# A fused block kernel: scale and shift of the first norm, order of loads and work up to the values, sums of modulation pieces

## The chip, the cores and the metric

One core of a Trainium2 chip runs the whole program in one launch. The metric is the device time of that launch in microseconds; lower is better. TensorE (PE) multiplies into PSUM, VectorE (DVE), ScalarE (ACT) and GpSimd (POOL) work elementwise, SyncE (SP) issues nearly all DMAs.

## The reference, cut to what matters

Two transformer blocks one after the other on 256 tokens of 1024 features, all in float32; the second puts 16 meta tokens in front. The change touches the beginning of the first block:

```python
cs = jax.nn.silu(c)
mod = cs @ ada_w[l] + ada_b[l]                       # 6 x 1024 values from c (1 x 1024)
shift1, scale1, gate1, shift2, scale2, gate2 = jnp.split(mod, N_MOD, axis=-1)
h = modulate(rmsnorm(x, norm1_g[l]), shift1, scale1) # h * (1 + scale) + shift
proj = h @ w_in[l]
qa, ka, va, qb, kb, vb, ga, gb = jnp.split(proj, offsets, axis=-1)
```

Behind it come window attention of 8 heads (`qa`, `ka`, `va`), causal attention of 8 heads (`qb`, `kb`, `vb`), both gated by sigmoids of `ga`, `gb`, an output projection, an MLP, and then the second block (four gated MLPs, a pooling mixer, a latent attention).

## The kernel before, in words

Activations lie with features on partitions: 8 feature tiles `kt` of 128, with 256 tokens as columns. Float32 matmuls with weights are made of three fast ones: weights and activations are each split into a rounded high part and a low part (the rest), and high x high, high x low and low x high are summed in PSUM.

**The stream of weights.** `weight_plan` cuts all weights into 443 chunks of at most 8 blocks of 128 x 128 (512 KB), in the order of use. `sync_program` (line 511 on) loads chunk `c` into `raw[c % 8]` once chunk `c - 8` is free. A chunk for matmuls is split: ScalarE writes the high part (`split_hi`, line 1009), VectorE the low part (`split_lo`, line 1342), into 5 slots `whi`/`wlo`; a slot is free when TensorE has finished with it. A chunk of `ada_w` is not split: VectorE multiplies it with values of silu(c), one scalar to a partition, and adds up (lines 1362 to 1371, and 1423 for the first stage); TensorE then sums over partitions with a product with a column of ones (line 612 in the first stage, line 600 in `mod_sum`). VectorE adds the bias (line 1376, `mod_out`).

**How far the splits run ahead** is fixed by `Plan`. For the weight chunk in use at stream position `c` it lists the chunks to be split within five positions of the stream; ScalarE goes up to the last of these, VectorE up to the one before it, at least its own:

```python
for i, c in enumerate(self.split):
    ahead = [number[k] for k in range(c, min(c + NRAW - LOADING, len(self.chunks))) if k in number][:AHEAD + 2]
    self.hi_to[i], self.lo_to[i] = ahead[-1], max(i, ahead[-1] - 1)
```

`splits(name)` calls this before a matmul group's own elementwise work.

**First stage.** ScalarE squares x (line 1050); TensorE sums the squares over features with a matrix of 1/1024 (line 619); ScalarE takes the root (1023), VectorE the reciprocal (1386): `rstd`. GpSimd forms y = x * rstd in 8 steps (line 1897). For each tile `kt`, in turn: the products of 8 row blocks of `ada_w` with silu(c), scale and shift side by side (256 columns), the first by ScalarE (1046), seven by VectorE (1423); two sums by TensorE (612); scale and shift values by VectorE (1426, 1427); h = y * gain + shift (ScalarE, 1064), its high part (1066), its low part (VectorE, 1440); the splits of the chunks of `w_in` that this tile needs. TensorE then adds this tile into 13 output tiles of 256 tokens, 39 matmuls (lines 640 to 642), in 7 PSUM banks: the group `qk`. The products of tile `kt + 2` stand ahead of tile `kt`'s splits and low part in VectorE's list.

Meanwhile GpSimd writes the row of position biases to DRAM and at once reads it back as a shifted table for 16 heads (2 MB, line 1899), which the first head needs (`shifts1`, line 1469).

**Values.** `va` (128 columns) and then `vb` (512 columns) are made with tokens on partitions (`token_major`, line 584): 8 tiles x 2 token halves x 3 matmuls each. The qk banks are copied out after the whole qk group. Then `mod_sum("mod4")`.

**Heads.** For head `i` of 16, TensorE's list is: scores of head i, the group `gate{i}` (24 matmuls), transposes of head i-1, values of head i-2. VectorE's list for head i is `shifts1`, a piece of `ada_w` products, `recip1`, `splits("gate{i}")`. Sums of mod5, 8, 9 and 6 stand behind heads 4, 8, 12 and 16; those of mod7, mod10 and mod11 stand behind `wout1`, `mlp_in7` and `mlp_out0`.

## Time and profile before

| | us |
|---|---|
| three runs | 1318.66, 1314.93, 1320.06 (median 1318.66) |
| profiled execution | 1321.37 |
| its span | 1320.0 |
| TensorE busy | 1257.1 (95%) |
| VectorE busy | 894.4 (68%) |
| ScalarE busy | 633.1 (48%) |
| mean granted TensorE clock | 0.974 |

The span is the time from the first to the last recorded work. A matmul is pipelined: its recorded length is longer than the interval to the next, so rates are read from the distance between starts. A product in full float32 shows as two passes. In the chain of waits each piece of time belongs to what the last instruction waited for at that time.

### The profile page before, as it was taken

How to read it: one execution, taken by the hardware profiler on the slowest of the kernel's cores; microseconds unless marked ns; L12 is line 12 of the kernel's file. 1: busy time of each engine (PE TensorE's matmuls, PEld its weight loads, DVE VectorE, ACT ScalarE, POOL GpSimd, SP SyncE). 2: the span in 40 equal slices, each digit the busy share in tenths (PEclk: the TensorE clock that was granted, in tenths of full speed). 3: DMA queues.
4: the chain of work that ended last, by engine and by line, in shares of the span. 5: the costliest groups of instructions: out<-in, count | busy, mean ns of one | idle time of the engine just before them, and what ended most of it. 6: DMA issues, size and time to landing. Idle time of an engine off the chain costs nothing.

```text
span 1320.0 us, 23814 instructions
## 1 busy us (share of the span) xinstructions
PE 1257.1 (95%) x9940; PEld 1221.1 (93%) x9940; DVE 894.4 (68%) x1275; ACT 633.1 (48%) x973; POOL 182.9 (14%) x181
## 2 busy tenths in 40 slices
PE   4999998999999999998799999989999999999996
PEld 3988998999999999998799999989999967999996
DVE  6968878777556766656866656776665563866653
ACT  4545544666444444544544444444454453644531
POOL 2014433000123000012300001400001310000022
PEclk7999999999999999999899999989999987999998
DMA  8956564656555555554245565355556531555540
GB/s 316 381 195 216 192 236 147 242 220 243 194 175 160 177 175 189 177 176 160 88 162 166 182 197 178 131 160 191 190 180 192 190 96 34 176 192 185 185 158 33
DMA packets 66995, 238.88 MB, mean 181 GB/s; under 512 B 7302, under 2 KB 9528, under 8 KB 66888
## 3 DMA queue, kind: packets, MB, share of 16 engines
q1 hardware_dynamic: 66296, 235.17, 53.1%
q0 software_dynamic: 592, 2.19, 0.5%
q8 instruction: 79, 1.29, 0.4%
q14 instruction: 28, 0.23, 0.1%
HBM read 236.26 MB, written 1.07 MB: 180 GB/s over the span
## 4 chain that ended last, share of the span: by engine, by line
PE 85%; DVE 10%; ACT 2%; issue 2%; POOL 1%; DMA 0%; SPq 0%; DVEq 0%; ACTq 0%
PE G L564 25%; PE G L565 25%; PE G L566 25%; DVE sb_wlo L1342 3%; DVE sb_hidf L1423 2%; PE G L584 1%; PE A L666 1%; DVE sb_rstd L1386 1%; PE A L619 1%; PE G L600 0%; DMA sb_X<-in_xT 0%; PE A L689 0%; DVE sb_xl L1843 0%; PE A L584 0%; PE A L676 0%
## 5 line engine op out<-in xcount | busy, mean ns | idle before, releaser
L1342 DVE TENSOR_TENSOR sb_wlo<-sb_raw,sb_whi 128x1024 fp32r<-128x1024 f32 x395 | 488.5, 1270 | 94.0 <-ACT sb_whi L1009 93.7
L564 PE MATMUL G<-sb_xh,sb_whi 128*128 128x256 f32 (+2 forms) x1764 | 503.0, 285 | 12.8 <-DVE sb_gu L1631 7.5
L565 PE MATMUL G<-sb_xl,sb_whi 128*128 128x256 f32 (+2 forms) x1764 | 502.0, 285 | 0.0
L566 PE MATMUL G<-sb_xh,sb_wlo 128*128 128x256 f32 (+2 forms) x1764 | 500.7, 284 | 0.0
L1009 ACT ACTIVATE sb_whi<-sb_raw 128x1024 fp32r<-128x1024 f32 x395 | 404.4, 1050 | 193.5 <-PE G L566 167.7
L564 PEld LDWEIGHTS G<-sb_xh,sb_whi 128*128 128x128 f32 x1764 | 333.8, 189 | 16.5 <-DVE sb_gu L1631 8.4
L566 PEld LDWEIGHTS G<-sb_xh,sb_wlo 128*128 128x128 f32 x1764 | 333.5, 189 | 0.0
L565 PEld LDWEIGHTS G<-sb_xl,sb_whi 128*128 128x128 f32 x1764 | 333.4, 189 | 0.1
L564 PE MATMUL G<-sb_hh,sb_whi 128*128 128x256 f32 (+1 forms) x1056 | 299.5, 284 | 7.1 <-DVE sb_X L1394 4.5
L566 PE MATMUL G<-sb_hh,sb_wlo 128*128 128x256 f32 (+1 forms) x1056 | 298.8, 283 | 0.0
L565 PE MATMUL G<-sb_hl,sb_whi 128*128 128x256 f32 (+1 forms) x992 | 280.3, 283 | 0.0
L564 PEld LDWEIGHTS G<-sb_hh,sb_whi 128*128 128x128 f32 x1056 | 199.2, 189 | 7.8 <-DVE sb_X L1394 4.6
L566 PEld LDWEIGHTS G<-sb_hh,sb_wlo 128*128 128x128 f32 x1056 | 199.2, 189 | 0.0
L565 PEld LDWEIGHTS G<-sb_hl,sb_whi 128*128 128x128 f32 x992 | 186.5, 188 | 0.0
L1193 ACT ACTIVATE sb_gu<-sb_gu 128x272 f32<-128x272 f32 (+1 forms) x88 | 37.4, 425 | 195.8 <-DVE sb_gu L1631 193.2
L1631 DVE TENSOR_TENSOR sb_gu<-G,sb_rstd 128x544 f32<-128x544 f32 (+1 forms) x84 | 59.4, 707 | 62.6 <-PE G L566 62.6
L1871 POOL TENSOR_TENSOR sb_sumsq<-sb_X 128x256 f32<-128x256 f32 (+1 forms) x6 | 3.7, 620 | 699.6 <-DVE sb_X L1394 699.6
L1635 DVE TENSOR_TENSOR sb_hidf<-sb_gu 128x272 f32<-128x272 f32 (+1 forms) x88 | 38.2, 434 | 50.6 <-ACT sb_gu L1193 50.6
L1638 DVE TENSOR_TENSOR sb_hl<-sb_hidf,sb_hh 128x272 fp32r<-128x272 f32 (+1 forms) x88 | 38.2, 434 | 43.2 <-ACT sb_hh L1195 43.2
L1195 ACT ACTIVATE sb_hh<-sb_hidf 128x272 fp32r<-128x272 f32 (+1 forms) x88 | 37.3, 424 | 50.3 <-DVE sb_hidf L1635 50.3
L1876 POOL TENSOR_TENSOR sb_sq<-sb_X 128x256 f32<-128x256 f32 (+1 forms) x42 | 33.0, 787 | 204.7 <-DVE sb_X L1394 204.7
L1879 POOL TENSOR_TENSOR sb_sumsq<-sb_sumsq,sb_sq 128x256 f32<-128x256 f32 (+1 forms) x43 | 47.4, 1102 | 3.4
(300 smaller groups left out, 1299.9 us busy)
## 6 DMA issues: line engine op xcount, KB each, us to landing
sb_raw<-in_wstream SPq DMA_DIRECT2D x443, 512.0 KB, 4.3
sb_bias<-bias_scratch POOLq DMA_DIRECT2D x1, 2048.0 KB, 14.0
sb_X<-in_xT SPq DMA_DIRECT2D x2, 512.0 KB, 6.4
out_T<-sb_X SPq DMA_DIRECT2D x4, 256.0 KB, 2.2
sb_con<-in_consts SPq DMA_DIRECT2D x1, 632.0 KB, 6.6
sb_vec<-in_vecs SPq DMA_DIRECT2D x1, 82.5 KB, 2.0
sb_X<-in_metaT POOLq DMA_DIRECT2D x1, 64.0 KB, 4.6
sb_boh<-in_bias_oh SPq DMA_DIRECT2D x1, 51.0 KB
```

Source lines behind the costliest of these rows:

```text
L564: e.matmul(out, w_h, xs, start=k0 + s.kt == 0, stop=False)
L565: e.matmul(out, w_h, xr, start=False, stop=False)
L566: m = e.matmul(out, w_l, xs, start=False, stop=k0 + s.kt == ktotal - 1)
L1009: e.activation(whi[:, i % NSPLIT, 0:w], raw[:, c % NRAW, 0:w], ACT.Copy).then_inc(hi_done, 1)
L1193: e.activation(gu[:, b, 0, 0:n], gu[:, b, 0, 0:n], ACT.Silu).then_inc(silu_done, 1)
L1195: e.activation(hh[:, j * n:(j + 1) * n], hidf[:, b, 0:n], ACT.Copy).then_inc(hid_hi, 1)
L1342: e.tensor_tensor(wlo[:, i % NSPLIT, 0:w], raw[:, c % NRAW, 0:w], f(whi[:, i % NSPLIT, 0:w]), ALU.subtract).then_inc(lo_done, 1)
L1631: e.tensor_tensor(gu[:, b, :, 0:n], G[plan.pair[name]][:, :, 0:n], rb, ALU.mult).then_inc(left_dve, 1)
L1635: e.tensor_tensor(hidf[:, b, 0:n], gu[:, b, 0, 0:n], gu[:, b, 1, 0:n], ALU.mult).then_inc(hid_mul, 1)
L1638: e.tensor_tensor(hl[:, sl], hidf[:, b, 0:n], f(hh[:, sl]), ALU.subtract).then_inc(hid_lo, 1)
L1876: e.tensor_tensor(s, src, src, ALU.mult).then_inc(sumsq_done, 1)
L1879: e.tensor_tensor(sumsq[:, cols], sumsq[:, cols], s, ALU.add).then_inc(sumsq_done, 1)
```

## The change

- `ada_w` for scale and shift of tiles 0 and 1 comes as four chunks `ada_p{kt}_{i}` (eight row blocks of one of the two), and TensorE multiplies them with silu(c) directly (`shift_scale_direct`). Tiles 2, (3, 4), (5, 6), 7 are `UNITS`; for a pair VectorE's products have 512 columns.
- Scale and shift values are formed by ScalarE. The squares are added by VectorE first and summed by one matmul. `rstd` is exp(-0.5 ln(mean + eps)), both on ScalarE.
- The order of chunks is: ada_p0_1, ada_p0_0, ada_p1_1, ada_p1_0, ada_h2_0, qk_0, ada_h2_1, qk_1, qk_2, four of unit (3, 4), qk_3 to 5, four of unit (5, 6), qk_6 to 8, two of unit (7,), qk_9 to 12; then ada4_0, v_0 to v_2, ada4_1, v_3 to v_5, ada4_2, v_6, v_7, ada4_3, ada5_0, gate0, ada5_1, gate1.
- The values are one group `v` of 5 blocks to a tile (8 chunks of 5 blocks), made in two halves of 320 columns.
- qk banks are copied out as each is finished. GpSimd forms y before it stores the bias row, and reads the table back only once the low part of qk chunk 11 is done.
- `mod_sum` transposes the four accumulated blocks; `mod_out` sums them over the columns and adds the bias. The third matmul of a head's values goes into the first.

The core of the diff (names of semaphores, PSUM places and copies left out):

```diff
+    def some_qk(n):
+        for i in range(done[0], done[0] + n):
+            group(f"qk_{i}", qk[i * CH:(i + 1) * CH], True)
+        done[0] += n
+
+    def unit(tiles):
+
+        per = CH // (2 * len(tiles))
+        for m in range(KT // per):
+            group(f"ada_h{tiles[0]}_{m}", [("ada_w", 0, _r(r * P), _r((i * KT + kt) * P)) for r in _r(per * m, per) for kt in tiles for i in (1, 0)], True)
+
+    for kt in range(PE_TILES):
+        for i in (1, 0):
+            group(f"ada_p{kt}_{i}", [("ada_w", 0, _r(r * P), _r((i * KT + kt) * P)) for r in range(KT)], True)
+    unit(UNITS[0])
+    groups.insert(len(groups) - 1, ("qk_0", qk[:CH], True))
+    done[0] = 1
+    some_qk(2)
...
+    unit(UNITS[1])
...
+    some_qk(3)
...
+    v_group = lambda kt: group(f"v_{kt}", [("w_in", 0, _r(kt * P), c) for c in [_r(o["va"])] + [_r(o["vb"] + j * P) for j in range(4)]], True)
+    for part, kts in enumerate(((0, 1, 2), (3, 4, 5), (6, 7), ())):
         ada(4, part)
-    group("va", [("w_in", 0, _r(kt * P), _r(o["va"])) for kt in range(KT)], True)
-    for part in (2, 3):
-        ada(4, part)
-    group("vb", [("w_in", 0, _r(kt * P), _r(o["vb"] + j * P)) for kt in range(KT) for j in range(4)], True)
+        for kt in kts:
+            v_group(kt)
...
@@ -597,60 +622,81 @@
                     if t % 4 == 0:
                         e.wait_ge(ada_total, ADA_ORDER.index(i + t // 4) + 1)
                     acc = ada_sets[ADA_SET[i + t // 4]][0][:, t % 4 * P:(t % 4 + 1) * P]
-                    m = e.matmul(out[:, 0, t:t + 1], acc, one_col[:, 0:1], start=True, stop=True)
+                    m = e.transpose(out[:, 0, t * P:(t + 1) * P], acc, ident)
...
+            def shift_scale_direct(kt):
+
                 if kt:
                     e.wait_ge(gain1_done, 2 * kt)
                 else:
-                    e.wait_ge(root_done, ROOT["norm1"])
-                for n in range(2):
...
-                    m = e.matmul(A[0][:, n:n + 1], acc1(kt)[:, n * P:(n + 1) * P], one_col[:, 0:1], start=True, stop=True)
+                    e.wait_ge(silu_c, 1)
+                for i in (1, 0):
+                    c = where[f"ada_p{kt}_{i}"][0][0]
+                    e.wait_ge(loaded[c % NRAW], 16 * (c // NRAW + 1))
+                    for r in range(KT):
+                        m = e.matmul(A[0][:, 1 - i:2 - i], raw[:, c % NRAW, r * P:(r + 1) * P], csil[:, r:r + 1], start=r == 0, stop=r == KT - 1)
+                    m.then_inc(sum1_half, 1)
+
+            def shift_scale_sum(u):
+
+                e.wait_ge(acc1_done, products_to(u, KT - 1))
+                e.wait_ge(gain1_done, 2 * UNITS[u][0])
+                for n in range(2 * len(UNITS[u])):
+                    m = e.matmul(A[0][:, n:n + 1], acc1(u)[:, n * P:(n + 1) * P], one_col[:, 0:1], start=True, stop=True)
                 m.then_inc(sum1_done, 1)
...
+            src1 = lambda kt: (xh[:, kt, COLS1], xl[:, kt, COLS1])
+            shift_scale_direct(0)
             e.wait_ge(consts_set, 5)
+            e.wait_ge(xsum_done, 4)
+            mean(0, COLS1, None, 1)
+            shift_scale_direct(1)
+            e.wait_ge(rows_in, 32)
+            e.matmul(G[1][0:HEADS1, 1, 0:BIASC], brow[:, :], boh[:, :], start=True, stop=True).then_inc(bias_made, 1)
+
+            sums_at = {(1, 0): 0, (2, 9): 1, (4, 9): 2, (6, 6): 3}
+            for s in steps["qk"]:
+                kt = s.kt
+                if (kt, s.t) in sums_at:
+                    shift_scale_sum(sums_at[kt, s.t])
+                if s.t == 0:
+                    e.wait_ge(xl_done, XSTAGE["h"] + kt + 1)
+                if (kt, s.t) == (0, 9):
+                    e.wait_ge(bias_row, 1)
+                if s.opens:
+                    e.wait_ge(lo_done, s.i + 1)
...
+                    m.then_inc(qk_bank, 1)
+                m = e.matmul(out, w_l, xh[:, kt, COLS1], start=False, stop=kt == KT - 1, skip_group_check=True)
+                if s.closes or s.j == QK_TILES * KT - 1:
...
+                s, last = steps["v"][5 * kt], steps["v"][5 * kt + 4]
+                e.wait_ge(lo_done, s.i + 1)
+                w_h, w_l = (w[:, s.i % NSPLIT, 0:640] for w in (whi, wlo))
+                for i in range(2):
+                    rows = slice(META + i * P, META + (i + 1) * P)
+                    for half in range(2):
+                        if kt == 0 and half == 0:
+                            e.wait_ge(qk_act, i + 1)
+                        elif kt == 0:
+                            e.wait_ge(qk_dve, i + 1)
+                        cols, out = slice(320 * half, 320 * half + 320), v_out[i][half]
+                        e.matmul(out, xh[:, kt, rows], w_h[:, cols], start=kt == 0, stop=False)
+                        e.matmul(out, xl[:, kt, rows], w_h[:, cols], start=False, stop=False)
+                        m = e.matmul(out, xh[:, kt, rows], w_l[:, cols], start=False, stop=kt == KT - 1)
+                m.then_inc(mm_done, 1)
             e.wait_ge(qk_act, 4)
             e.wait_ge(qk_dve, 3)
+            e.wait_ge(con_in, 16)
             mod_sum("mod4", 4)
 
...
-                e.matmul(o[:, P:SEQ], vv(0), pT1[:, b, 0:P], start=True, stop=False)
-                e.matmul(o[:, P:SEQ], vv(1), pT1[:, b, P:SEQ], start=False, stop=True)
-                e.matmul(o[:, 0:P], vv(0), pT1[:, b, SEQ:384], start=True, stop=True).then_inc(valued1, 1)
+                e.matmul(o[:, 0:SEQ], vv(0), pT1[:, b, 0:SEQ], start=True, stop=False, skip_group_check=True)
+                e.matmul(o[:, P:SEQ], vv(1), pT1[:, b, SEQ:384], start=False, stop=True, skip_group_check=True).then_inc(valued1, 1)
...
-            e.activation(warm[:, 1:2], eps_c[:, 0:1], ACT.Sqrt)
...
+            e.activation(warm[:, 1:2], eps_c[:, 0:1], ACT.Ln)
...
+            def shift_scale(kt, n=0):
+                e.activation(g1m[:, kt:kt + 1], A[0][:, 2 * n:2 * n + 1], ACT.Identity, bias=gb[:, kt:kt + 1], scale=V("norm1_g", kt)).then_inc(gain1_done, 1)
+                e.activation(mod[:, kt:kt + 1], A[0][:, 2 * n + 1:2 * n + 2], ACT.Identity, bias=V("ada_b", kt)).then_inc(gain1_done, 1)
+
...
+            for n in range(4):
+                e.wait_ge((x_in, x_rest)[n // 2], 16)
+                e.activation(sig[:, 2 * n:2 * n + 2, :], X[:, 2 * n:2 * n + 2, COLS1], ACT.Square).then_inc(xsq_done, 1)
+            e.wait_ge(gb_done, 1)
+            e.wait_ge(sum1_half, 2)
+            shift_scale(0)
+            e.wait_ge(mean_done, MEAN["norm1"])
+            e.activation(root[:, COLS1], A[1][:, 0:SEQ], ACT.Ln, bias=eps_c[:, 0:1]).then_inc(root_done, 1)
+            preload(ACT.Exp)
+            e.wait_ge(root_done, ROOT["norm1"])
+            e.activation(rstd[:, COLS1], root[:, COLS1], ACT.Exp, scale=-0.5).then_inc(rstd_done, 1)
+            split_hi(0)
+            x_high(0)
+            split_hi(1)
+            e.wait_ge(sum1_half, 4)
+            shift_scale(1)
+            x_high(1)
+            e.wait_ge(bias_made, 1)
+            e.activation(brows[:, :], G[1][0:HEADS1, 1, 0:BIASC], ACT.Copy).then_inc(bias_row, 1)
+            split_hi(2)
+            first_product(1)
+            unit_shift_scale(0)
+            x_high(2)
+            split_hi(5)
+            first_product(2)
+            unit_shift_scale(1)
+            x_high(3)
+            x_high(4)
+            split_hi(8)
+            first_product(3)
+            unit_shift_scale(2)
+            x_high(5)
+            x_high(6)
+            split_hi(10)
+            unit_shift_scale(3)
+            x_high(7)
+            split_hi(13)
...
+            qk_copy(0)
+            split_hi(14)
+            qk_copy(2)
+            split_hi(15)
+            qk_copy(4)
+            qk_copy(6)
+            splits("v")
+            e.wait_ge(mm_done, ended["v"])
+            e.activation(vtok[:, 0, 0:320], A[2][:, 0:320], ACT.Copy).then_inc(v0_act, 1)
+            e.activation(vtok[:, 1, 0:320], G[plan.pair["v"]][:, 0, 0:320], ACT.Copy).then_inc(left_act, 1)
...
-                e.tensor_tensor(mod[:, 4 * i:4 * (i + n)], G[plan.pair[name]][:, 0, 0:4 * n], V("ada_b", 4 * i, 4 * n), ALU.add).then_inc(left_dve, 1)
+                e.tensor_reduce(mod[:, 4 * i:4 * i + 4], G[plan.pair[name]][:, 0, :].rearrange("p (t d) -> p t d", t=4), AX_X, ALU.add).then_inc(left_dve, 1)
+                e.wait_ge(left_dve, plan.left_dve[name])
+                e.tensor_tensor(mod[:, 4 * i:4 * i + 4], mod[:, 4 * i:4 * i + 4], V("ada_b", 4 * i, 4), ALU.add).then_inc(mod_set, 1)
...
+            for n in range(1, 4):
+                e.wait_ge(xsq_done, n + 1)
+                if n > 1:
+                    e.wait_ge(xsum_done, n - 1)
+                e.tensor_tensor(sig[:, 0:2, :], sig[:, 0:2, :], sig[:, 2 * n:2 * n + 2, :], ALU.add).then_inc(xsum_done, 1)
+            e.wait_ge(xsum_done, 3)
+            e.tensor_tensor(sumsq[:, COLS1], sig[:, 0, :], sig[:, 1, :], ALU.add).then_inc(xsum_done, 1)
+            e.wait_ge(silu_c, 1)
+            products(0, 0, 4)
+            split_lo(0)
+            x_low(0)
+            split_lo(1)
+            products(0, 4, 8)
+            x_low(1)
+            split_lo(2)
+            products(1, 1, 4)
+            split_lo(3)
+            x_low(2)
+            products(1, 4, 8)
+            split_lo(5)
+            x_low(3)
+            x_low(4)
+            split_lo(6)
+            products(2, 1, 4)
+            split_lo(7)
+            products(2, 4, 8)
+            split_lo(8)
+            x_low(5)
+            x_low(6)
+            products(3, 1, 8)
+            split_lo(9)
+            split_lo(10)
+            x_low(7)
+            split_lo(12)
...
-            for part in (0, 1):
-                ada_piece(4, part)
-            split_lo(plan.lo_to[steps["va"][0].i])
-            e.wait_ge(mm_done, ended["qk"])
-            for i in (1, 3, 5):
-                qk_copy(i)
-            splits("va")
-            for part in (2, 3):
-                ada_piece(4, part)
-            splits("vb")
-            e.wait_ge(mm_done, ended["vb"])
-            e.tensor_copy(vtok[:, 1, P:5 * P], G[plan.pair["vb"]][:, 1, :]).then_inc(left_dve, 1)
+            ada_piece(4, 0)
+            split_lo(13)
+            qk_copy(1)
+            qk_copy(3)
+            split_lo(14)
+            qk_copy(5)
+            split_lo(15)
+            ada_piece(4, 1)
+            split_lo(18)
+            ada_piece(4, 2)
+            split_lo(20)
+            ada_piece(4, 3)
+            splits("v")
+            e.wait_ge(mm_done, ended["v"])
+            e.tensor_copy(vtok[:, 0, 320:640], A[3][:, 0:320]).then_inc(v0_dve, 1)
+            e.tensor_copy(vtok[:, 1, 320:640], G[plan.pair["v"]][:, 1, 0:320]).then_inc(left_dve, 1)
             mod_out("mod4")
...
+            e.wait_ge(rstd_done, RSTD["norm1"])
+            for kt in range(KT):
+                e.tensor_tensor(sig[:, KT + kt, :], X[:, kt, COLS1], rstd[:, COLS1], ALU.mult).then_inc(y_done, 1)
             e.wait_ge(bias_row, 1)
             e.dma_start(scratch[:, 0:BIASC], brows[:, :]).then_inc(rows_out, 16)
             hankel = bass.AP(scratch.tensor, 0, [[1, P], [512, HEADS1], [1, SEQ]])
-            e.wait_ge(rstd_done, RSTD["norm1"])
```

## Rows read from the trace of the kernel before

**Rows 1.** the page: busy time and share of each engine, DMA issues.

```profile
...
PE 1257.1 (95%) x9940; PEld 1221.1 (93%) x9940; DVE 894.4 (68%) x1275; ACT 633.1 (48%) x973; POOL 182.9 (14%) x181
...
sb_bias<-bias_scratch POOLq DMA_DIRECT2D x1, 2048.0 KB, 14.0
...
```

**Rows 2.** the chain of waits, 0 to 120 us: start us, us, what.

```profile
...
2.12 5.92 DMA sb_X<-in_xT
...
8.85 6.65 PE A L619 x16
...
57.66 0.39 PE G L640
71.66 5.31 PE A L584 x48
76.97 11.17 PE G L584 x48
88.14 0.79 PE G L600 x8
...
```

**Rows 3.** TensorE's instructions: start us, us, line, operation, out<-in, [idle before <-releaser].

```profile
...
16.17 0.61 PE L612 MATMUL A<-sb_one_col,sb_hidf 128*128 128x1 f32 x4
...
27.68 0.58 PE L640 MATMUL G<-sb_xh,sb_whi 128*128 128x256 f32 x1 [1.52 <-DVE sb_xl L1440]
...
69.34 0.28 PE L640 MATMUL A<-sb_xh,sb_whi 128*128 128x256 f32 x1
...
71.38 0.28 PE L642 MATMUL A<-sb_xh,sb_wlo 128*128 128x256 f32 x1
...
```

**Rows 4.** VectorE's instructions, 0 to 93 us.

```profile
...
16.04 1.75 DVE L1386 RECIPROCAL sb_rstd<-sb_root 128x256 f32<-128x256 f32 x1 [1.03 <-ACT sb_root L1023]
...
18.77 6.00 DVE L1423 SCALAR_TENSOR_TENSOR sb_hidf<-sb_raw,sb_csil,sb_hidf 128x256 f32<-128x256 f32 x7 [0.82 <-ACT sb_hidf L1046]
...
24.95 2.34 DVE L1342 TENSOR_TENSOR sb_wlo<-sb_raw,sb_whi 128x1024 fp32r<-128x1024 f32 x2
...
27.55 3.66 DVE L1423 SCALAR_TENSOR_TENSOR sb_hidf<-sb_raw,sb_csil,sb_hidf 128x256 f32<-128x256 f32 x7
...
```

**Rows 5.** ScalarE's instructions, 0 to 93 us.

```profile
...
15.53 0.47 ACT L1023 ACTIVATE sb_root<-A,sb_eps_c 128x256 f32<-128x256 f32 x1 [4.29 <-PE A L619]
...
16.78 1.28 ACT L1019 ACT_TABLE_LOAD   x1
...
20.47 0.58 ACT L1064 ACTIVATE sb_tmp<-sb_sig,sb_mod,sb_g1m 128x256 f32<-128x256 f32 x1
21.09 0.42 ACT L1066 ACTIVATE sb_xh<-sb_tmp 128x256 fp32r<-128x256 f32 x1
...
```

**Rows 6.** groups by line, 0 to 93 us: count | busy us, mean ns.

```profile
...
L1897 POOL TENSOR_TENSOR sb_sig<-sb_X,sb_rstd 128x256 f32<-128x256 f32 x8 | 6.6, 858 | 0.1
...
L1365 DVE SCALAR_TENSOR_TENSOR sb_gu<-sb_raw,sb_csil,sb_gu 128x512 f32<-128x512 f32 x6 | 4.1, 746 | 0.0
...
```

**Rows 7.** windows: length, busy us (count) of each engine, granted clock, DMA share, GB/s.

```profile
...
15.00:20.00 5.00, 2.63 (x13) 1.52 (x11) 3.12 (x6) 4.17 (x7) 2.81 (x4) 0.83 1.03 409
...
25.00:30.00 5.00, 3.30 (x15) 3.25 (x16) 4.79 (x9) 1.53 (x3) 0.67 (x1) 0.50 0.83 255
...
216.00:218.00 2.00, 2.00 (x13) 2.00 (x12) 1.92 (x2) 0.31 (x1) 1.92 (x3) 0.56 0.50 203
...
348.00:350.00 2.00, 2.00 (x19) 2.00 (x19) 1.68 (x3) 2.00 (x4) 1.92 (x4) 1.00 0.03 8
...
```

**Rows 8.** the chain of waits, 84 to 98 us: start us, us, what.

```profile
...
89.81 0.42 DVE sb_sc L1469
...
94.12 0.39 PE G L564
...
```

**Rows 9.** TensorE after the sums of mod7 and mod11.

```profile
...
214.87 0.39 PE L564 MATMUL G<-sb_hh,sb_whi 128*128 128x256 f32 x1 [1.97 <-DVE sb_X L1394]
...
347.78 0.38 PE L564 MATMUL G<-sb_hh,sb_whi 128*128 128x256 f32 x1 [2.51 <-DVE sb_X L1394]
...
```

198 lines of the change are left out of this document (76 added, 122 removed).

## The prediction, as put on record before the changed kernel was run

> **What bounds the kernel now.** Read first the shares: TensorE is busy 95% of the span [rows 1]. Time is won only where TensorE idles or does work it could spare. The chain of waits over the first 120 us shows where that is: x lands at 8.0, TensorE sums squares until 15.5, and then the chain is VectorE's until 57.7; from there it is TensorE back to back: qk to 71.7, va 5.3 us, vb 11.2 us, sums of mod4 0.8 us, first scores [rows 2]. TensorE's first qk matmul is at 27.7, at the half clock [rows 3, 7]. From 27.7 to 71.5 are 43.8 us; 312 matmuls at 0.120 (17 intervals from 69.34 to 71.38 [rows 3]) are 37.4, the rest is slow clock and waits for VectorE. Each feature tile costs VectorE seven products, one or two low splits and an x low part [rows 4].
>
> **The start.** The direct sums of tile 0 read raw chunks 0 and 1. ScalarE used chunk 0 at 5.0; I start there. A one-column product is two passes: four passes took 0.61 with their tail [rows 3], 0.11 each warm, about 0.22 cold. The 16 matmuls of the squares ran at 0.42 a pass [rows 2], twice the 0.21 I expect of the full clock, though the clock column reads 1.00; so TensorE is cold until some 5.7 us into its first work. 32 passes: done at 11.7. The squares end at 10.6 as before; VectorE's four adds (0.6 each, 0.35 the last) end at 11.9; the mean is now two passes: 12.5. Ln 0.5, table load 1.3, warm 0.1, Exp 0.5 [rows 5]: rstd at 15.0, against 17.8 (sqrt, then 1.75 of reciprocal [rows 4]). Tile 1's direct sums (3.5) and the bias matmul run under that, until 17.
> Table load: the trace has one between square root and the next Exp [rows 5], so I charge 1.3. (The Trainium skill, "ScalarE: Activation LUTs", section "Table sets: the hidden batching unit", says one set holds both ln and exp, so one load serves both; by that rstd stands at 13.7 and all behind it up to 1.3 earlier. No row here shows that set.)
> GpSimd forms y in eight steps of 0.83 while VectorE works. VectorE's seven products beside it took 6.0, without it 3.66 [rows 4]: +0.33 an operation. Seven VectorE operations now fall beside it: +2.3. (The Trainium skill, "SBUF — State Buffer", section "Who interferes with whom", has a VectorE operation with two SBUF inputs and a GpSimd one exclude each other for a whole instruction. 0.49 and 0.83 in turn would be 1.3 a product; the row shows 0.84, so the trace does not bear out full exclusion. By the rule the start would lose some 3 us more.)
> With y0 at 15.8, high split 1.0, two steps of x high 1.04 [rows 5], low split 1.15 [rows 4] and x low 0.35, plus 0.5 of the above: qk starts at 18.3, 9.4 earlier.
>
> **The qk stage**, walked in the order written. A step (tile, three matmuls) 0.355; low split 1.15; product of 512 columns 0.76 (0.746 busy [rows 6], dependent), of 256 columns 0.51 [rows 4]; x high 1.04, to TensorE 1.5; shift/scale on ScalarE 0.2 an operation; a sum 0.5 a tile.
> - kt 0: 18.3 to 23.0. VectorE: low 1 to 19.8, products(0,4..8) at 0.84 to 23.1, x low 1, low 2 to 24.65. kt 1 starts 23.65, reaches low 3 at 27.5, which is done at 28.1 behind three products: idle 0.6.
> - kt 2: low 4 is queued behind products(1,4..8) (28.4 to 31.5): 32.65, wanted at 31.0: idle 1.7. Sum 1 stands at tile 9 (0.95); kt 2 ends 36.1. x high 3 cannot start before that sum: x low 3 at 36.9, idle 0.8.
> - kt 3, 4: low 6, 7 in time; sum 2 at (4,9) waits for products(2) (46.2): idle 1.4; then x high 5: 0.85.
> - kt 5: low 9 is behind seven products of the last unit: these start at 50.4 after x low 6, end 54.0, low 9 at 55.2; wanted at 51.9: idle 3.3.
> - kt 6, 7: sum 3 at 60.0, x high 7, high 11, low 11 at 63.7; wanted 61.4: idle 2.3. End of qk 69.5.
> 51.2 us: 37.4 of matmuls, 2.9 of sums, 10.9 idle, where before 43.8 held 6.4 of sums, slow clock and idle. Against 71.5: **-2.0**. Bounds: TensorE without any wait would end at 18.3+37.4+2.4=58 (-13), but VectorE's 34 us of this list plus the handovers don't allow it; I keep 4 us either way.
> Loads: 512 KB at 409 GB/s [rows 7] is 1.28. A chunk is asked for eight back: 14 when products(0) end (23.1), 20 when products(1) end (31.5), 25 at 42: each lands 3 to 4 us later, before ScalarE wants it. The bias table (2 MB, 14.0 us to landing [rows 1], during which the weights came at 255 GB/s [rows 7]) no longer takes bandwidth here: that removes a wait of ScalarE of 7 us, part of the old stalls. It now starts at 63.7 and lands by some 80; wanted at 85. Costed at nothing; without that margin it is one for one.
>
> **Values.** 96 matmuls before: 48 of 128 columns in 5.3, 48 of 512 in 11.2 [rows 2]: 0.111 and 0.232. Now 96 of 320. Between 256 columns (0.120) and 512 the time goes with columns, 0.452 ns each: 0.145, in all 13.9 against 16.5: **-2.6** (bounds 0.111 and 0.232 each: -5.8 to +5.8; the neighbours on both sides fix it). Chunks of five blocks cost the splits 0.8 instead of 1.15; VectorE is 3 us ahead. The copies of qk run in the last kt.
>
> **Sums of mod pieces.** Eight passes become four transposes: 0.79 to 0.9 [rows 2] down to 0.44. Mod4: **-0.45**. In the head stage TensorE is the bound: mod5, 8, 9, 6 **-1.8**; VectorE's +0.75 (a 512-column reduction, a wait, an add) replaces idle time there. Mod7, 10 and 11 stand before a residual or evacuation that TensorE awaits (2.5 us at mod11 [rows 9]): -0.45+0.75 each, **+0.9**. Values of two matmuls in place of three: same columns, 0.
>
> **Head 0: the new wait.** VectorE's low splits run ahead to lo_to: the last weight chunk within five stream chunks, less one. Before, the last vb chunk (37) saw gate0 (39) and gate1 (41): gate0's low part was done during vb. Now the stream ends v7 (39), ada4_3, ada5_0, gate0 (42), ada5_1, gate1 (44): v7 sees only gate0, lo_to is v7 itself. So gate0's low split stands behind shifts1(0), an ada piece and recip1(0). Before, the split of gate1 stood there: shifts began at 89.81, that split released TensorE at 94.12, 4.3 later [rows 8]. TensorE's queue is scores1(0), gate0, scores1(1), gate1, transposes; all wait. Shifts also start 0.5 later (two copies 0.9, reduction 0.65, add 0.16 against 0.97). Idle 4.8, less the 0.55 that gate1 cost: **+4.25**. The bound below is 0 (if the split runs ahead after all).
>
> **Clock.** The granted clock fell to 0.5 around the idle time at 17 to 27 and again at 216 after a wait of 2.0 us; after the 2.5 us at mod11 it did not [rows 7, 9]. From 27.7 it took 3.9 us of work to come back: 2.0 us lost. For the 4.8 us of head 0 I take **+2.0** (bounds 0 and 3.4). For the 3.3 of kt 5 perhaps 1.7, which I set against the table load that may go.
>
> **Sum.** -2.0 -2.6 -0.45 -1.8 +0.9 +4.25 +2.0 = **+0.3**. The profiled run took 1321.37 (span 1320.0, 1.4 around it), 2.7 above the median of 1318.66 of the three runs; the difference carries over: 1321.7 profiled, **1319.0** as a median.
>
> **Rivals.**
> 1. *The early start is kept.* If VectorE and ScalarE hand over better than I walk (one table load, waits at kt 2 and kt 5 half as long), qk ends 5 to 6 earlier: 1312, with a warm clock 1311. For: 11 us of idle rest on my placing of products; against: the placing is the written order. 0.18.
> 2. *No stall at head 0.* Then -4.25 -2.0: 1312.7. Against: the lo_to rule above. 0.07.
> 3. *Slower: the clock.* TensorE now has gaps of 1.7, 3.3, 2.3 and 4.8, plus 1.3 before kt 0. Each that drops the clock costs up to 2.0, and behind each late sum stands ScalarE. Four drops with little slack: +8 against +2: about 1326. It decides from the third drop on (over +6.6). For: one drop after 2.0 us idle; against: none after 2.5. 0.10.
> 4. *The bias table lands late*: it shares the queues with v3 to v7; 1 us per us beyond 85; 8 us late would give 1327. 0.03.
> 5. *GpSimd and VectorE take whole turns* at the start: 7 operations at 0.49+0.83 instead of 0.84 are 3.4 more: 1322.4. The products beside y speak against it [rows 4]. 0.02. (This is the SBUF page's rule above.)
> 6. *One table load serves both*: 1317.7, a variant inside the forecast, 0.4 of it. (The ScalarE page's rule above.)
> 7. *It changes less than it says* (gain in qk near 0, rest as above): 1321, inside the forecast's own case.
> The forecast, with 6 and 7, has 0.60. About 0.5% (6.6 us) is what a measurement can tell from no change. Below 1312.1: most of rival 1 and half of 2, 0.18; above 1325.3: 0.11; between 0.71. Range: 1311 to 1325.
>
> **What would show it.** qk's first matmul near 18.3; rstd 15.0 (13.7 without a load); gaps at low 4, low 9, low 11 with VectorE's split as releaser; qk's end 69.5; v matmuls 0.145 apart; first scores near 84; then TensorE idle 4 to 5 us before gate0, released by the low split; clock 0.5 behind it. Wrong if gate0 follows the scores at once, if qk ends before 66 or after 73, or if a DMA releases ScalarE's splits for long.

## The result: 0.8% slower, outside the range

| kernel | median us (lowest to highest, runs) | profiled execution, its span | mean clock |
|---|---|---|---|
| before | 1317.42 (1314.93 to 1320.06, 4) | 1321.37, 1320.0 | 0.974 |
| changed | 1328.72 (1326.36 to 1333.02, 4) | 1329.67, 1328.0 | 0.977 |

Ratio 1.0082, 95% interval 1.0053 to 1.0111: some 11 us slower. Forecast were 1319.0 with a range of 1311 to 1325. A second measurement of both kernels side by side (experiment 11) gave 1327.68 against 1318.07, ratio 1.0073 (1.0057 to 1.0089).

### The profile after

TensorE's share is unchanged, and the bias table takes as long to land as before [rows 1]:

```profile
...
PE 1260.1 (95%) x9918; PEld 1227.0 (92%) x9918; DVE 890.5 (67%) x1247; ACT 634.8 (48%) x988; POOL 185.9 (14%) x181
...
sb_bias<-bias_scratch POOLq DMA_DIRECT2D x1, 2048.0 KB, 14.0
...
```

TensorE at the start (start us, us, then line, operation, out<-in, and in brackets the idle time before it). In the kernel before, the squares and the first qk matmul stand in [rows 2, 3]:

```profile
...
5.29 6.96 PE L639 MATMUL A<-sb_csil,sb_raw 128*128 128x1 f32 x32 [5.29 <-DMA sb_raw<-in_wstream]
12.29 1.19 PE L617 MATMUL A<-sb_sumsq,sb_mean_ones 128*128 128x256 f32 x2
13.28 6.83 PE L639 MATMUL A<-sb_csil,sb_raw 128*128 128x1 f32 x32
20.03 1.46 PE L657 MATMUL G<-sb_boh,sb_brow 34*16 34x384 f32 x2
21.42 0.58 PE L672 MATMUL A<-sb_xh,sb_whi 128*128 128x256 f32 x1
...
```

Both groups of 32 one-column passes (the direct sums of tiles 0 and 1, direct(0) and direct(1)) take 0.21 us a pass, the second no faster than the first. TensorE has no idle time from 5.29 on, so its queue sets the start: qk begins at 21.42, 6.3 earlier than before. The elementwise work for it was done at 19.27 (the low part of x, on VectorE). The granted clock is full only from 25.7, so tile 0 of qk runs mostly at the half clock.

ScalarE at the root [rows 5]. The table load stands between Ln (L1120) and Exp (L1123):

```profile
...
13.52 0.47 ACT L1120 ACTIVATE sb_root<-A,sb_eps_c 128x256 f32<-128x256 f32 x1 [0.67 <-PE A L617]
14.02 1.28 ACT L1066 ACT_TABLE_LOAD   x1
15.42 0.40 ACT L1123 ACTIVATE sb_rstd<-sb_root 128x256 f32<-128x256 f32 x1
...
```

GpSimd's eight products beside VectorE, where before one took 858 ns [rows 6] (a group by line: count | busy us, mean ns | idle before it):

```profile
...
L2012 POOL TENSOR_TENSOR sb_sig<-sb_X,sb_rstd 128x256 f32<-128x256 f32 x8 | 8.2, 1064 | 15.4 <-ACT sb_rstd L1123 15.4
...
```

Six of the eight took 0.72 to 0.92 us, as all eight did before. The two others took 1.71: they ran while VectorE made the low parts of chunks 0 and 1, of which the first took 1.60 us in place of 1.21.

TensorE's waits from there on, in order ("low 4" is the wait for VectorE's low part of qk chunk 4): low 4, low 9, low 11, the end of v with the sum of mod4 and the first scores, gate0 in head 0, the output projection, the sum of mod7 and what follows it, what follows the sum of mod10, and what follows the sum of mod11 [rows 2, 8, 9]. Two of 0.8 to 0.9 us, at 51.1 and 54.5, are left out:

```profile
...
37.17 0.39 PE L672 MATMUL G<-sb_xh,sb_whi 128*128 128x256 f32 x1 [1.65 <-DVE sb_wlo L1429]
...
60.53 0.58 PE L672 MATMUL G<-sb_xh,sb_whi 128*128 128x256 f32 x1 [3.26 <-DVE sb_wlo L1429]
...
72.05 0.39 PE L672 MATMUL G<-sb_xh,sb_whi 128*128 128x256 f32 x1 [2.42 <-DVE sb_wlo L1429]
...
93.42 0.60 PE L625 MATMUL G<-sb_con,sb_gu 128*128 128x128 f32 x4
93.95 0.70 PE L712 MATMUL A<-sb_qk 64*128 64x256 f32 x2
...
99.63 0.55 PE L589 MATMUL G<-sb_xh,sb_whi 128*128 128x256 f32 x1 [4.76 <-DVE sb_wlo L1429]
...
216.13 0.36 PE L589 MATMUL G<-sb_hh,sb_whi 128*128 128x256 f32 x1 [1.90 <-DVE sb_wlo L1429]
...
223.36 0.60 PE L625 MATMUL G<-sb_con,sb_sc 128*128 128x128 f32 x4
...
226.18 0.39 PE L589 MATMUL G<-sb_hh,sb_whi 128*128 128x256 f32 x1 [2.23 <-DVE sb_X L1483]
...
287.62 0.39 PE L589 MATMUL G<-sb_xh,sb_whi 128*128 128x258 f32 x1 [1.65 <-DVE sb_hidf L1696]
...
359.85 0.39 PE L589 MATMUL G<-sb_hh,sb_whi 128*128 128x256 f32 x1 [3.25 <-DVE sb_X L1483]
...
```

Windows around four of them, as in [rows 7] (length; busy us and count of TensorE, its weight loads, VectorE, ScalarE, GpSimd; granted clock; DMA share, GB/s):

```profile
...
38.00:42.00 4.00, 4.00 (x26) 3.90 (x25) 0.68 (x2) 2.62 (x9) 0.00 (x0) 0.67 0.91 327
...
59.00:67.00 8.00, 6.47 (x31) 6.47 (x32) 2.61 (x3) 0.00 (x0) 0.00 (x0) 0.57 0.70 254
97.00:104.00 7.00, 4.37 (x20) 4.40 (x21) 3.13 (x6) 2.86 (x7) 3.46 (x2) 0.53 0.54 162
...
360.00:363.00 3.00, 3.00 (x16) 3.00 (x17) 2.64 (x4) 2.16 (x5) 2.92 (x4) 0.54 0.00 0
...
```

Every wait shown but one has half clock (1.2 GHz) at it or behind it: 3.4 us from 39.4, 6.8 from 59.9, 3.4 from 73.5, 6.8 from 97.4, then 3.4 each from 216.9, 227.1 and 360.2. The wait of 1.65 us at 287.6 has none.

VectorE in head 0 shows why gate0 waits. The ada piece (L1449) and the reciprocal (L1606) run before the two low splits, of gate0 and gate1:

```profile
...
96.67 0.88 DVE L1449 TENSOR_SCALAR sb_hidf<-sb_raw,sb_csil 128x512 f32<-128x512 f32 x2
...
98.19 0.17 DVE L1606 RECIPROCAL sb_stat<-sb_stat 128x2 f32<-128x2 f32 x1
98.28 2.34 DVE L1429 TENSOR_TENSOR sb_wlo<-sb_raw,sb_whi 128x1024 fp32r<-128x1024 f32 x2
...
```

Where the time went is read from the starts of the same operations in every profile: VectorE's evacuation of the scores of heads 0 and 1, the first and third residual tile after attention (between them stands mod7's sum), the first residual tile behind the sums of mod10 and mod11, and the first gated product of the layer behind that, in us:

| profile | scores 0 | scores 1 | resid 0 | resid 2 | resid 8 | gated 0 |
|---|---|---|---|---|---|---|
| before | 89.81 | 93.99 | 208.32 | 213.94 | 346.86 | 434.99 |
| before again (8) | 88.91 | 93.09 | 207.43 | 213.05 | 345.96 | 435.67 |
| changed | 95.23 | 105.64 | 218.17 | 225.26 | 358.93 | 448.63 |
| changed again (11) | 93.94 | 104.25 | 216.76 | 223.86 | 357.51 | 447.83 |
| 1 gate0 ahead | 95.30 | 100.16 | 214.02 | 221.11 | 354.79 | 444.49 |
| 2 wide matmuls | 95.90 | 105.59 | 218.09 | 224.42 | 358.09 | 448.40 |
| 3 late order | 85.30 | 95.14 | 207.63 | 214.73 | 348.40 | 437.94 |
| 4 rest alone | 86.88 | 91.74 | 205.72 | 212.81 | 346.50 | 436.20 |
| 5 late, gates, sums | 85.71 | 89.77 | 202.26 | 207.88 | 340.75 | 430.45 |
| 6 high 3 ahead | 84.78 | 88.61 | 201.09 | 207.84 | 340.74 | 430.46 |
| 12 the same again | 84.04 | 88.09 | 200.55 | 206.17 | 338.95 | 428.67 |
| 7 rest, best | 87.20 | 91.03 | 203.56 | 210.27 | 343.19 | 432.90 |
| 9 bias first | 85.62 | 89.45 | 201.91 | 207.55 | 340.44 | 430.16 |
| 10 gates only | 85.21 | 89.26 | 201.76 | 208.88 | 342.54 | 432.82 |
| 13 warm, bridged | 82.60 | 86.43 | 198.91 | 204.52 | 337.41 | 427.12 |

The changed kernel against the one before: 5.4 us lost by the first scores, 6.2 in head 0, 1.8 regained over the heads, 1.5 lost between resid 0 and resid 2, 0.8 at mod10 and mod11 together, and 1.6 in the half clock at 360. Not all of the 1.5 is mod7's sum: the half clock from 216.9 to 220.3 stands ahead of that sum (223.36), behind the wait of 1.90 us at 216.13, which the kernel before has as well, without half clock behind it. Experiment 2 has the same sum with no half clock there, and loses 0.7 (6.33 us from resid 0 to resid 2, against 5.62 before and 7.09 in the changed kernel):

```profile
...
221.78 0.60 PE L625 MATMUL G<-sb_con,sb_sc 128*128 128x128 f32 x4
...
225.35 0.39 PE L589 MATMUL G<-sb_hh,sb_whi 128*128 128x256 f32 x1 [2.97 <-DVE sb_X L1489]
...
```

In all the changed kernel is 13.6 us later at gated 0, more than the 11 of the medians. From gated 0 to the end the kernel before took 885.0 us in its first profile and 877.5 in its second, the changed kernel 879.4 and 881.2, so differences behind that point are not the change's.

### The profile page after: what moved, and what is told of

It reads as the page before. It is cut to its first block, busy times and chain, and to the rows that moved or that the text cites. A ratio compares the mean times of both kernels' runs of the same rounds, so it can differ in the third digit from the quotient of the medians.

```text
span 1328.0 us, 23775 instructions
## 1 busy us (share of the span) xinstructions
PE 1260.1 (95%) x9918; PEld 1227.0 (92%) x9918; DVE 890.5 (67%) x1247; ACT 634.8 (48%) x988; POOL 185.9 (14%) x181
## 3 DMA queue, kind: packets, MB, share of 16 engines
q8 instruction: 78, 1.28, 0.4%
## 4 chain that ended last, share of the span: by engine, by line
PE 82%; DVE 9%; ACT 2%; issue 2%; POOL 1%; DVEq 0%; ACTq 0%
PE G L589 25%; PE G L590 25%; PE G L591 25%; DVE sb_wlo L1429 2%; DVE sb_rstd L1475 1%; PE A L737 1%; PE A L712 1%; ACT sb_whi L1056 1%; DVE sb_xl L1961 0%; ACT sb_p L1392 0%; DVE sb_X L1824 0%; PE A L589 0%; PE A L723 0%; PE G L1007 0%; POOL sb_sumsq L1997 0%
## 5 line engine op out<-in xcount | busy, mean ns | idle before, releaser
L1429 DVE TENSOR_TENSOR sb_wlo<-sb_raw,sb_whi 128x1024 fp32r<-128x1024 f32 (+1 forms) x398 | 489.1, 1262 | 97.9 <-ACT sb_whi L1056 97.7
L1056 ACT ACTIVATE sb_whi<-sb_raw 128x1024 fp32r<-128x1024 f32 (+1 forms) x398 | 404.5, 1043 | 183.0 <-PE G L591 169.7
```

Of the source, the lines that this page charges most:

```text
L1056: e.activation(whi[:, i % NSPLIT, 0:w], raw[:, c % NRAW, 0:w], ACT.Copy).then_inc(hi_done, 1)
L1429: e.tensor_tensor(wlo[:, i % NSPLIT, 0:w], raw[:, c % NRAW, 0:w], f(whi[:, i % NSPLIT, 0:w]), ALU.subtract).then_inc(lo_done, 1)
```

## The experiments

Ratios are to the kernel before on the same chip, with 95% intervals; chips differ between experiments (1 to 4, 5 to 12, 13), so compare the ratios rather than the times across these groups. Line numbers are the experiment's own.

**1. gate0's low split ahead.** In VectorE's program:

```
...
             splits("v")
+            split_lo(21)
...
```

> The changed kernel with one more low split on VectorE before it waits for the values (the low part of gate0). Theory A (the split queued behind head 0's softmax costs the 10.4 us between the first two score evacuations, 4.8 of them idle and the rest half clock): that distance falls to about 4.2, the total by 6.2 to 6.7 us, and the clock column shows no 0.5 at 97 to 104. Rival: head 0 is bound by the chain shift, exponential, reciprocal anyway; then TensorE idles before gate1 instead and the total falls by 2 at most.

Measured: 1326.32 us, ratio 1.0052 (1.0034 to 1.0070). The stall before gate0 is gone, but now gate1 waits:

```profile
...
100.30 0.58 PE L589 MATMUL G<-sb_xh,sb_whi 128*128 128x256 f32 x1 [1.72 <-DVE sb_wlo L1429]
...
```

with the clock at half for 3.4 us from 100. The second scores follow the first by 4.86 us (10.41 in the changed kernel, about 4.2 expected); of the 6.2 us, 4.2 came back by resid 0. The ratio fell by 0.3%, some 4 us, less than the 6.2 to 6.7 expected. The cause of the stall is shown; it had a second wait right behind it.

**2. Wide matmuls for the clock.** Five of 384 columns ahead of the direct sums, four behind the bias matmul, their result unused.

> The changed kernel with wide filler matmuls (128x384 float32, result not used): 5 before the direct sums, 4 between the bias row and the first qk matmul. Theory B (TensorE stayed at half clock through 64 one-column passes and kt 0, and that made qk late): qk starts by 19.5 instead of 21.4, kt 0 runs at 0.12 a matmul instead of 0.21, kt 1 starts at 24.6 instead of 28.6, the first score evacuation 4 us or more earlier than 95.2. Rival (the handovers of VectorE and ScalarE bound the stage): kt 1 starts 4 earlier but the gaps at low 4 and low 9 grow by as much, and the first scores come at most 1.5 earlier. Open: whether the one-column passes run at 0.11 once the wide ones have raised the clock, or fall back to 0.21.

Measured: 1330.92 us, ratio 1.0101 (1.0071 to 1.0130).

```profile
...
1.40 4.89 PE L654 MATMUL G<-sb_mean_ones 128*128 128x384 f32 x10 [1.40 <-DVE sb_mean_ones L1502]
6.12 3.63 PE L639 MATMUL A<-sb_csil,sb_raw 128*128 128x1 f32 x32
12.10 1.22 PE L617 MATMUL A<-sb_sumsq,sb_mean_ones 128*128 128x256 f32 x2 [2.35 <-DVE sb_sumsq L1532]
13.12 6.83 PE L639 MATMUL A<-sb_csil,sb_raw 128*128 128x1 f32 x32
...
21.26 4.55 PE L654 MATMUL G<-sb_mean_ones 128*128 128x384 f32 x8
25.35 0.57 PE L678 MATMUL A<-sb_xh,sb_whi 128*128 128x256 f32 x1
...
```

Behind wide work direct(0)'s passes take 0.11 us. Then TensorE idles 2.35 us for VectorE's adds, the clock falls, and it stays at half for 13.7 us from 11.1, though TensorE works without a break from 12.10, for 6.8 us of that in one-column passes. So the clock fell in an idle stretch, and direct(1) ran its whole length at half. The last fillers ran at half clock and pushed qk to 25.35 (19.5 expected), which ate the gain: the first scores come at 95.90, no earlier. Whether the handovers would have eaten it otherwise, the rival, this run cannot say.

**3. Order of the late tiles.** ScalarE takes high 12 where it took high 10; VectorE takes low 9 between the products of the last unit:

```
...
-            x_low(5)
-            x_low(6)
-            products(3, 1, 8)
-            split_lo(9)
-            split_lo(10)
+            products(3, 1, 5)
+            x_low(5)
+            x_low(6)
+            split_lo(9)
+            products(3, 5, 8)
+            split_lo(12)
...
```

> The changed kernel with another order at tiles 5 to 7 alone: four products of the last unit before x low 5, low 9 before the remaining three, high and low parts of chunks 11 and 12 before tile 7's scale and shift. Theory C (the idle 3.3 us before low 9 and 2.4 before low 11, and the half clock from 60 to 66.7 behind the first, come from the order alone): both gaps go, no slow stretch there, first score evacuation 7 to 8 us earlier (about 87.5). Rival (the clock falls anyway or the last unit's sum, wanted at tile (6,6), now waits for the products): 3 us or less.

Measured: 1320.11 us, ratio 1.0002 (0.9982 to 1.0022); first scores 9.9 us earlier than in the changed kernel.

```profile
...
58.00:66.00 8.00, 8.00 (x70) 8.00 (x70) 6.27 (x9) 3.74 (x9) 1.21 (x1) 1.00 0.99 363
...
```

TensorE is busy throughout that window, at the full clock. The two gaps were 3.26 and 2.42 us, 5.7 together. The other 4.2 fit the half clock behind them. From the start of kt 5 to the end of qk the changed kernel takes 24.99 us (54.52 to 79.51), this one 14.60 (54.99 to 69.59). Of the 10.4 between them 5.7 are the two waits; the rest is 4.7, and an estimate of what the 10.2 us of half clock cost is 4.8 (half of the 9.6 in which TensorE was busy). This one order was most of the loss: the ratio falls from 1.0082 to 1.0002.

**4. The rest of the change, with the first stage of before.** V in halves of 320 columns, chunks of five blocks, qk banks copied out as they end, transposed sums, two matmuls for a head's values, gate0's split ahead.

> The kernel before with the other parts of the change and without its first-stage order: values in halves of 320 columns, five-block chunks, qk banks copied out as they end, sums of mod pieces by transposes, two matmuls for a head's values; gate0's low part ahead as in e1. The forecast's terms for these parts: -2.6 values, -0.45 mod4, -1.8 and +0.9 for the other sums: 3.5 to 4 us below the kernel before, first score evacuation at 87.3 (89.8 before, of which +0.5 for VectorE's longer end of stage). If the first-stage order is what made the change slower, this one is faster than before; if the values or sums did, it is not.

Measured: 1318.21 us, ratio 0.9996 (0.9978 to 1.0014). First scores at 86.88 (87.3 expected), 2.9 earlier than in the first profile of before and 2.0 earlier than in its second; of the 2.9, 2.2 are lost by the scores of head 4, at gate1 and the half clock behind it, and what stands behind the heads gives back more. The expected gain of 3.5 to 4 us in the time is not there: the interval holds 1.

**5. Three mends together:** the order of 3; gate0 as in 1 and gate1's parts likewise (ScalarE's high part before the first exponentials, VectorE's low part behind the first shifts); mod7, 10 and 11 summed by one-column products again. In head 0, `recip1` also stands ahead of the `ada_w` piece.

```
...
-                    m = e.transpose(out[:, 0, t * P:(t + 1) * P], acc, ident)
+                    if i in (7, 10, 11):
+                        m = e.matmul(out[:, 0, t:t + 1], acc, one_col[:, 0:1], start=True, stop=True)
...
                     shifts1(i)
-                    ada_piece(*ADA_HEADS[i])
-                    recip1(i)
+                    if i == 0:
+                        split_lo(22)
+                        recip1(i)
+                        ada_piece(*ADA_HEADS[i])
...
```

> The changed kernel with four edits, each aimed at a wait its trace shows: the late-tile order of the third experiment; the low split of gate0 straight behind the v splits and, new, gate1's (ScalarE's high part ahead of the first exponentials, VectorE's low part straight behind the first shifts); and mod7, mod10 and mod11 again summed by one-column products with one add. Theory (the loss is handovers, each doubled by the half clock behind it): against the late-order kernel the stall in head 0 goes, with the clock drop behind it (-6.2 us), and the three sums that stand before a waiting evacuation give back 1 us each (-3.0 to -3.4, the half clock behind mod7 included). Against the kernel before, the first scores stay 4.5 us earlier, the fourth head's are 4 to 5 us earlier, and mod10's evacuation is 6 to 8 us earlier: 1311 to 1313 us, ratio 0.994 to 0.996. Rival A (TensorE's late stages take back what the start gains, whatever the handovers): ratio 0.999 to 1.001. Rival B (the clock falls in these stages whatever stands in front of it): the stall is gone, but half-clock stretches still stand near 90, 205 and 350 us; 1315 to 1317 us.

Measured: 1314.65 us, ratio 0.9989 (0.9966 to 1.0011). In head 0 VectorE now does:

```profile
...
87.15 1.22 DVE L1433 TENSOR_TENSOR sb_wlo<-sb_raw,sb_whi 128x1024 fp32r<-128x1024 f32 x1
...
88.76 1.08 DVE L1453 TENSOR_SCALAR sb_hidf<-sb_raw,sb_csil 128x512 f32<-128x512 f32 x2
...
```

and head 1's scores follow head 0's by 4.06 us (10.41 in the changed kernel, 4.18 before). The profile has 6.1 us less than before at resid 0, and still at resid 8. The medians keep 2.5 of it, with an interval that reaches past 1: the stages behind vary by several us (8). The 1311 to 1313 us expected are missed, and the ratio is within 0.0001 of rival A's range. Rival B is borne out in part: near 90 no half clock is left, but stretches of 3.4 us still stand at 208.8 and 341.9, behind waits of 1.96 and 2.52 us that the kernel before has too.

**6. High split 3 ahead** of the shift and scale of tile 2, on ScalarE.

> The previous kernel, and ScalarE takes the high part of chunk 3 before the shift and scale of tile 2 instead of behind it. Theory (VectorE's idle time near 28 us and TensorE's wait at low split 4 near 37 us come from that high part standing behind a wait for the sum): VectorE's 2.9 us of idle shrink, TensorE's gap of 1.65 us goes, and if the clock drop near 38 us was answered by that gap it goes too: 2 to 4 us less than the previous kernel, 1308 to 1311. Rival (the gap only moves: x high 3 and the sum of unit 0 then come late by as much): within 1 us of the previous kernel.

Measured: 1312.82 us, ratio 0.9971 (0.9959 to 0.9983). The gap of 1.7 us before low 4 and the half clock behind it are gone, and the values start 2.3 us earlier than in 5 (66.98 against 69.28). Yet the first scores come only 0.9 earlier, and the median 1.8, with intervals that overlap; expected were 2 to 4. Where the rest goes the profile shows:

```profile
...
80.95 1.06 ACT L1059 ACTIVATE sb_whi<-sb_raw 128x1024 fp32r<-128x1024 f32 x1 [3.09 <-DMA sb_raw<-in_wstream]
...
82.04 1.23 DVE L1434 TENSOR_TENSOR sb_wlo<-sb_raw,sb_whi 128x1024 fp32r<-128x1024 f32 x1 [1.27 <-ACT sb_whi L1059]
83.18 0.48 DVE L1585 COPY sb_vtok<-A 128x320 f32<-128x320 f32 x1
...
```

The values end at 81.54, but VectorE copies them only at 83.18: gate0's low split, now ahead of the copies, waits for gate0's weights, with the DMA share at 1.03 and 408 GB/s from 74 to 81. With the early stage mended, the loads are the next limit there.

This profile also has half clock from 199.6, which 5 has not, behind the same gap:

```profile
...
199.05 0.36 PE L589 MATMUL G<-sb_hh,sb_whi 128*128 128x256 f32 x1 [1.89 <-DVE sb_wlo L1434]
...
199.00:203.00 4.00, 3.95 (x21) 3.98 (x22) 3.76 (x6) 1.40 (x4) 1.28 (x2) 0.58 1.00 379
...
```

and in 5:

```profile
...
200.22 0.35 PE L589 MATMUL G<-sb_hh,sb_whi 128*128 128x256 f32 x1 [1.89 <-DVE sb_wlo L1433]
...
200.00:204.00 4.00, 3.78 (x32) 3.81 (x33) 3.75 (x7) 1.40 (x4) 1.12 (x2) 1.00 0.95 370
...
```

**7. The first stage of before, with the rest in its mended form** (4 with the gate1 and the sums of 5). "The first kernel of this call" is that of 5.

> The first stage exactly as in the kernel before (root by Sqrt and reciprocal, all sums by accumulated products, its loads); behind it all the rest of the change: v in halves of 320 columns, chunks of five blocks, transposed sums for mod4, 5, 8, 9, 6, values of two matmuls, with the gates and mod7, mod10, mod11 mended as in the first kernel of this call. Theory: first scores 2.9 us earlier than before (as measured with the fourth experiment), the gap before gate1 and its half clock gone (-2.5), mod5, 8, 9, 6 -1.8, nothing given back at mod7, 10, 11: 5 to 7 us under the kernel before at mod10, 1312 to 1315 us. Set against the first kernel of this call it gives what the new first stage is worth with its order mended: the theory says 0 to 2 us. Rival (the new first stage is a gain of several us once its order is right): this kernel at 1316 or more with the first one at 1312.

Measured: 1315.57 us, ratio 0.9980 (0.9960 to 1.0001). Against 5 at resid 0 the new first stage is worth 1.3 us (0 to 2 expected), against 6 it is 2.5. In the medians it is 0.9 and 2.8, with overlapping intervals, so its worth in the time is not shown.

**8. The kernel before, once more.**

> The kernel before, unaltered, for a second profile of it. Question: do its half-clock stretches stand at the same places. Theory (a stretch is answered by what the kernel does there): again 13.7 us at 18, 3.4 at 216, 10.2 at 626, 6.8 at 872; none near 227 or 348. The stretch of 27 us at 1080, twice to four times as long as in all kernels since, is chance and will be 7 to 17 us here. Rival (the stretches are drawn by chance everywhere): different places all through.

Measured: 1314.53 us (one run). The early stretches are near where they were (19.7, 214.3, 623.9, 873.0), the first of them shorter (10.2 us, not 13.7), with one more, from 347.4, that was not expected; the one of 27 us is 3.4 us, less than the 7 to 17 expected. Windows of the first profile of before, then of the second:

```profile
...
347.00:350.00 3.00, 2.22 (x19) 2.22 (x20) 2.44 (x5) 2.57 (x5) 2.43 (x4) 1.00 0.02 5
...
1085.00:1105.00 20.00, 20.00 (x63) 11.61 (x62) 9.12 (x29) 6.93 (x19) 0.00 (x0) 0.50 0.18 53
...
```

```profile
...
347.00:350.00 3.00, 3.00 (x16) 3.00 (x17) 2.62 (x4) 2.18 (x5) 2.92 (x4) 0.57 0.03 5
...
1085.00:1105.00 20.00, 17.50 (x103) 12.70 (x102) 10.33 (x32) 7.78 (x20) 0.00 (x0) 0.91 0.20 55
...
```

So the half clock behind mod11's sum (1.6 us) is no mark of the change, and a single profile can be off by several us: 0.9 by the first scores (88.91 against 89.81) and 7.5 behind gated 0.

**9. Bias row first.** Its inputs are loaded first and its matmul stands ahead of the direct sums; the copies out of the pair bank go first.

> The sixth experiment's kernel (late-tile order, gates ahead, three column sums, high split 3 ahead) with two more edits: the bias row's small inputs are loaded first and its matmul stands before the direct sums, in TensorE's idle first 5 us, instead of between direct(1) and the first qk matmul (1.4 us there); and both engines copy the half of v that lies in the pair bank first, since gate0 waits for that bank (1.3 us of idle before gate0). Theory (the start is bound by TensorE's queue, and gate0 by the order of two copies): first qk matmul at 20.0 to 20.3 in place of 21.4, gate0's first matmul 0.4 us closer to the scores, 1 to 2 us off the time against the sixth kernel: 1311 to 1312, ratio to before 0.995 to 0.9965. Rival (VectorE sets the pace right behind: low split 3, the product sums): the first 1.4 us are gone again by tile 3, and the time is within 0.5 us of the sixth kernel's.

Measured: 1311.45 us, ratio 0.9947 (0.9932 to 0.9962), beside 1313.49 for 12 on the same chip; the intervals overlap. The mechanism did not work: the small loads landed only by 4.44, the direct sums began at 5.83, the mean at 14.09 (12.29 in the changed kernel), and qk began at 21.76, no earlier (20.0 to 20.3 expected). The other edit did what it should: TensorE idles 0.35 us before gate0, where it was 1.34 in 6 and 0.65 in 12. The first scores come later than in 6 and 12. So the median is where it was expected, but not by the mechanism named for the start: that is luck, and whether the 2 us against 12 are the edits' doing stays open. It is the fastest median of all, and clearly below the kernel before and the changed one.

**10. Gates and order, transposed sums kept** (5 without its sums).

> The changed kernel with the late-tile order and both gates ahead, all modulation sums by transposes as in the change: the fifth experiment's kernel less its three column sums. Theory (a transposed sum is 0.45 us cheaper where TensorE is the bound, but costs VectorE 0.75 us more where an evacuation is awaited): up to mod6 the same as the fifth kernel; then later by 1.0 to 1.5 us at mod7 (some of it the clock), 0.4 at mod10, 0.4 at mod11, in all 2 to 3.5 us, ratio to before 0.999 to 1.001. Rival (the three sums matter only through the clock's chance): within 1 us of the fifth kernel in the stretches between the clock's drops.

Measured: 1315.99 us, ratio 0.9979 (0.9968 to 0.9990). From 0.5 us ahead of 5 at resid 0 it falls 1.0 behind at resid 2, 1.8 at resid 8, 2.4 at the gated product: 2.9 in all. Only about half of it is the three sums'. Of the 1.5 by resid 2, 0.8 is the half clock from 200.1, ahead of mod7's sum, behind a wait of 1.90 us that 5 has too, without it; mod10 and mod11 cost 0.8; the last 0.6 is a difference that the two profiles of the changed kernel show as well (89.70 and 90.32 us from resid 8 to gated 0). And the ratio is no higher than that of 5 (0.9979 against 0.9989), where more was expected: the time does not show the sums. What one sum costs is seen in the idle time behind mod11's:

```profile
...
343.46 0.58 PE L589 MATMUL G<-sb_hh,sb_whi 128*128 128x256 f32 x1 [3.24 <-DVE sb_X L1484]
...
```

against 2.52 in 5. The 0.72 more is VectorE's longer evacuation; TensorE's sum is 0.35 shorter (0.60 against 0.95).

**11 and 12. The changed kernel and 6, again, on one chip.**

> The changed kernel itself once more, on the same chip as the others of this call, with a second profile. Theory: 1326 to 1329 us, ratio 1.007 to 1.009; first scores 5.4 us later than before, the second head's scores another 6.2 us; half-clock stretches again at the gaps before low split 9 and in head 0, while those far behind (at 227 and 360) may be elsewhere or missing, since the two profiles of the kernel before differ there as well. Rival (the stretch at 60 was chance): it is missing and the first scores come 2 to 3 us earlier.

> The sixth experiment's kernel once more, beside the first kernel of this call and beside the changed kernel on one chip. Expected 1312 to 1314 us, ratio to before 0.996 to 0.998, 14 to 16 us under the changed kernel. Against a ratio of 1.000 or more the gains seen in its first profile would be the profile's chance.

Measured: 1327.68 us, ratio 1.0073 (1.0057 to 1.0089), and 1313.49 us, ratio 0.9969 (0.9952 to 0.9986). All seven early stretches of half clock of the changed kernel are there again; only their lengths differ at low 4 (6.8 us, not 3.4) and low 9 (3.4, not 6.8). The first scores are 5.0 later than in before's second profile (expected 5.4), the second 6.1 more. Both medians are where they were expected; the kernel of 6 is 14.2 us under the changed one.

**13. A warm TensorE without idle time:** 6 with wide matmuls ahead of direct(0), between it and the mean, and behind the bias row.

```
...
+            wide_fill(5)
             shift_scale_direct(0)
...
+            wide_fill(4)
...
+            wide_fill(3)
...
```

> The sixth experiment's kernel with wide matmuls (384 columns, their result unused) wherever TensorE would idle before the first qk matmul: five ahead of the direct sums (in its idle first 5 us), four between direct(0) and the mean, three behind the bias matmul. In the second experiment the five in front made direct(0)'s 32 passes run at 0.11 us in place of 0.21, but TensorE then idled 2.35 us, the clock fell at 11.1, and direct(1) ran at 0.21 again. Theory (the forecast's start at 18.3 failed only because nothing wide kept TensorE at the full clock): both direct sums at 0.11 a pass, direct(1) done at 16.5, bias 0.7 more, first qk matmul at 18.6 to 19.3 and all of kt 0 at 0.12: kt 0 ends at about 24, 4 us earlier than in the sixth kernel; of that VectorE's later handovers leave 1 to 3 us at the first scores (81.5 to 83.5). Rival A (one-column passes lose the full clock even with no idle time around them): direct(1) at 0.21 in part, first qk matmul at 20 to 22, the last three fillers slow: 0 to 2 us later than the sixth kernel. Rival B (VectorE sets the pace from tile 1 on): kt 0 ends 4 us earlier, kt 1 or kt 2 waits for it, and the first scores stand within 0.5 us of the sixth kernel's 84.0 to 84.8.

Measured: 1313.98 us, ratio 0.9972 (0.9943 to 1.0002).

```profile
...
6.41 3.63 PE L642 MATMUL A<-sb_csil,sb_raw 128*128 128x1 f32 x32
9.90 2.83 PE L657 MATMUL G<-sb_mean_ones 128*128 128x384 f32 x8
12.56 0.69 PE L617 MATMUL A<-sb_sumsq,sb_mean_ones 128*128 128x256 f32 x2
13.09 3.63 PE L642 MATMUL A<-sb_csil,sb_raw 128*128 128x1 f32 x32
17.76 0.81 PE L666 MATMUL G<-sb_boh,sb_brow 34*16 34x384 f32 x2 [1.05 <-DMA sb_brow<-in_bias_rows]
18.51 3.86 PE L657 MATMUL G<-sb_mean_ones 128*128 128x384 f32 x6
21.91 0.57 PE L682 MATMUL A<-sb_xh,sb_whi 128*128 128x256 f32 x1
...
```

Both direct sums now run at 0.11 a pass, the second done at 16.7, as the prediction had it (17 with the bias row). So one-column passes do not lose the full clock by themselves (rival A). Then the bias row's load is late, the clock falls at 18.5, and the last fillers take 3.9 us: qk begins at 21.91, not at 18.6 to 19.3. x low 0 was done at 19.15. Even so the first scores come at 82.60 (81.5 to 83.5 expected), 1.4 to 2.2 earlier than in 12 and 6. A gain in the median is not shown.

## Why the prediction was wrong, step by step

- **The start: failed first.** "TensorE is cold until some 5.7 us into its first work", then 0.11 a pass: that carried the first 32 direct passes to 11.7 and TensorE's queue to 17, ahead of the elementwise chain, from which 18.3 for qk was worked out. Measured were 0.21 a pass throughout: the chain was ready at 19.27, the queue only at 21.42. The clock stayed at half until 25.7, so kt 0 and its sum took 6.98 us where 5.35 were forecast. I had taken the change from 0.42 to 0.21 among wide matmuls and applied it to passes of one column, which had stood at the half clock, 0.21, all along (2). With wide work ahead and no idle time, the forecast rate appears (13).
- **rstd** at 15.0, measured 15.8, of which 0.5 is the mean at the half clock (1.19 us, against 0.69 in 13); the table load was charged, rightly. (The Trainium skill, "ScalarE: Activation LUTs", section "Table sets: the hidden batching unit", has ln and exp in one set. The trace does not agree: a load of 1.28 us stands between them.)
- **GpSimd beside VectorE**: forecast 0.84 us a product; the four beside it took 0.94, 0.77, 0.77 and 0.77 (L1514), and started 0.86 to 1.05 apart, not the 1.3 of whole turns. Rival 5 did not happen. The low splits were another case: there GpSimd took 1.71 us, and the split 1.60.
- **The gaps at low 4, low 9, low 11**: forecast 1.7, 3.3, 2.3; measured 1.65, 3.26, 2.42. For these the walk through the written order was good to 0.12 us. All waits of qk together were forecast at 10.9 and came to 9.0.
- **The clock behind the gaps: failed, and cost most.** For these three gaps the sum charges nothing; 1.7 was set against a table load that might go. Behind them the half clock stood for 13.6 us, of which some 6.5 are lost (an estimate: half of what TensorE was busy in them). Qk ended at 79.51, not 69.5, past its own sign of being wrong (73): 3.1 by the start, 1.6 in kt 0, and 5.3 behind, where the half clock outweighs 1.9 less of waiting. So where the sum has -2.0 for qk, the runs have +7.9 (79.51 against 71.66). The first scores came at 95.23, not near 84; taking away the last two gaps alone brought 9.9 us (3), some 4.2 of them clock. The error was to price the clock gap by gap where I looked for it (head 0) and not for the others. (The price itself was read a little low: from 27.7 the half clock stood 4.2 us in the kernel before, not 3.9.) Rival 3, the clock, "about 1326" from the third drop on, is what happened; it had 0.10, and "about 1326" lay outside the stated range (its own prices, +8 against +2, give 1325).
- **Values**: 13.9 forecast, about 14.1 measured; the matmuls stand 0.147 apart, forecast 0.145.
- **Head 0**: +4.25 and +2.0 forecast. Idle 4.76, and the second scores 6.23 later against the first, where 6.25 were forecast: by the mechanism named (1, 5), though so close a match is partly luck, since the clock's share had bounds of 0 and 3.4.
- **Sums in the heads**: -1.8 for mod5, 8, 9, 6; from scores 4 to resid 0 -1.83 (99.31 before, 97.48 after).
- **Sums of mod7, 10, 11**: +0.9 forecast by counting the instructions. Idle time behind mod11's sum rose by 0.74 and the sum fell by 0.35, so +0.39 a sum, and 0.8 for mod10 and mod11 together; mod7's cost 0.7, read where no half clock stands ahead of it (2). That makes 1.5 for the three, in place of 0.9.
- **Bias table**: landed 14.0 us after its issue; nothing waited for it. Rival 4 did not happen.

In sum: the mechanisms of head 0 and of the sums were right, the three large waits in qk were right in place and size, and what turned "no change" into 11 us was TensorE's clock, at the start and behind the waits. That the half clock comes with the waits is shown by 3 and 1, where it went or shrank with them; why one wait is followed by it and another is not stays open (below).

## What to carry to other kernels

Where TensorE is the bound, price a wait of the size seen here (1.65 to 4.8 us) with the half clock that may stand behind it (3.4 to 6.8 us of it, half of that lost), and look for an order that closes it before adding anything else: here one reordering of splits was worth 9.9 us at the first scores and 0.8% of the time. A split that moves behind other work in an engine's written order is a wait for whoever reads it. Take two profiles of the kernel before, since stretches of half clock far behind the change differed by several us between runs of the same program, and read a cost where no such stretch stands in one profile alone.

## What had not been expected of the hardware

- Matmuls of one column run at 0.21 us a pass on the half clock and 0.11 on the full clock. The clock stayed at half through 6.8 us of them between other work (2), and at full through 3.6 us of them, twice, right behind wide matmuls (13).
- The same wait is followed by half clock in one profile and not in another. The one of 1.88 to 1.90 us in the output projection (216.13 in the changed kernel) had it behind it in 8 of the 15 profiles. The one behind mod11's sum, 2.51 us, had it in the second profile of the kernel before and not in the first.
- Nor does the length alone decide. The waits of 1.65 to 1.69 us at low 4 were followed by half clock in all 7 profiles that have them, those of 1.65 us behind mod10's sum (287.62) in none of 7. Of 34 waits of 2.2 us or more between 28 and 440 us, in all profiles, 33 were followed by it.
- GpSimd's products took 0.72 us alone, 0.90 to 0.92 beside VectorE's products, and 1.71 beside its low splits of 1024 columns, one of which took 1.60 us for 1.21.
